# A hybrid decoder layer on one core: output projection by column halves, ring slots loaded during it, normalised rows stored once

## The chip, the cores and the metric

The kernel runs on one core of one Trainium2 chip. The metric is the device time of one launch in microseconds; the medians below are over several launches of the same program. The engines are TensorE (PE; its weight loads are listed as PEld), VectorE (DVE), ScalarE (ACT), GpSimd (POOL) and SyncE (SP, which here issues nearly all transfers). They run their own instruction streams and wait for one another by semaphores.

## What is computed

One layer on x of 512 rows x 1024, all in float32:

```
h = rmsnorm(x, g_mix);  p = h @ w_in                      # 1024 -> 2304 columns
attn = sliding_window_attention(q, k, v, sinks)           # 8 heads x 64, window 128
conv = short_conv(b_gate, c_gate, x_in, conv_w)           # 512 columns, width 3
mix = concat([rmsnorm(attn, g_attn_out), rmsnorm(conv, g_conv_out)])
x = x + mix @ w_out                                       # the output projection
h = rmsnorm(x, g_ffn)
x = x + moe(h, ...)       # top 4 of 32 experts, each 1024 -> 2048 -> 1024, clamped SwiGLU
out = rmsnorm(x, g_final)
```

The experts' weights are 32 x 12 MiB, 403 MB. Each is read once.

## The kernel before

**Stages.** The 512 rows are four row tiles of 128 (TB = 4, index t). First come the norm, the input projection, and attention and convolution in turns, up to about 150 us. Then the output projection with the second norm, the router and the ranks of the tokens within their experts; then 32 experts one after another; then the sum of four expert rows per token and the last norm. The order of every engine's work is written out by hand; there is no scheduler.

**Output projection.** Weights and mixed activations are split in a high and a low part, and three products are summed (high x high, high x low, low x high). For one row tile t and one half n of the 1024 output columns these are 8 chunks of 128 rows of w_out x 3 = 24 matmuls with 512 columns. The accumulators are PSUM banks 2n (attention half) and 2n + 1 (conv half). `out_first` does tile 0, both halves, with the products in another order and the sums of squares (`group_sums`) between them; `out_proj(t, n)` does one half of tile 1, 2 or 3. DVE's `residual(t, n)` adds the result to X. When both halves of a tile are in X, ACT takes the sum of squares (`row_std`), DVE normalises (`second_norm`), PE transposes (`turn_h2`), ACT and DVE copy the two halves of the transposed tile (`turned_h2`), PE multiplies with the router weights (`router`), DVE finds the four chosen experts (`select`), PE sums ranks (`rank`), and DVE takes them over (`place`, `gates`). PE's order is, for t = 1, 2, 3: out_proj(t, 0), turn_h2(t - 1), rank(t - 2), out_proj(t, 1), router(t - 1); then turn_h2(3), rank(2), router(3), rank(3). After that the token lists of the first two experts are summed on PE (`tok_static`, L1163), and POOL fetches their rows with an indirect DMA (L1709).

**Normalised rows in DRAM.** `h2_rows` holds each normalised row four times, once per chosen expert: ACT stores each tile once (L1507, semaphore h2_stored) and then three more copies (L1508, h2_copied). Expert slot lists hold row numbers 4 x token + k, which serve both to fetch h2 rows and to scatter expert results to `expert_rows`. POOL writes the lists with 16 indirect transfers (L1734), reads them back in six (L1739, L1741) and turns row numbers into half and quarter rows (L1745). The third expert's rows and all later ones are fetched through them (L1700, L1703).

**The ring.** Expert weights go through a ring of 16 slots of 1 MiB (2048 floats in each of 128 partitions). Slots 0 to 7 lie in `ring1`, 8 to 11 in `ring2`, 12 to 14 in `mixer`, 15 in `early`. The first product of an expert takes 8 slots (loaded in pairs, L416), the second takes 4 (L421). SP's order is w1 of experts 0 and 1, w2 of expert 0, w1 of expert 2, w2 of expert 1 and so on; for each load after the first 16 slots it waits for PE to have used up the slot (`slot_used`). Until the experts begin, the same memory holds other things: `ring2` the rows of w_out (later their low parts), slots 4 to 7 the high parts, `mixer` q, k, v, gates, attention and conv results, `early` temporaries. So the first 16 slots are gated (`load`, L427): slots 0 to 3 wait for the input projection, 4 to 7 for the end of the output projection (oproj_done 8), 8 to 15 for the first fetched rows (rows_in).

**Experts.** "Big" experts (18 of 32) have 96 rows per pass, small ones 64. PE does for expert i: first product of i, transposition of the rows of i + 1, second product of i - 1, transposition of the activations of i.

Of the kernel before, what the change touches and what calls it, by code (L numbers as in the profile page):

```python
# [59 lines left out]
W_OUT_EARLY = tuple(k for k in range(KT) if k not in W_OUT_LATE)  # L60


W_OUT_PLACES = dict(zip(W_OUT_EARLY + W_OUT_LATE, (6, 7, 4, 5, 0, 1, 2, 3)))

# [10 lines left out]
def layer_kernel(nc, x, g_mix, w_in, conv_w, sinks, g_attn_out, g_conv_out, w_out,  # L75
                 g_ffn, w_router, b_router, w1, b1, w2, b2, g_final, out):
    ctx = ExitStack()
    with ctx:
# [11 lines left out]
        h2_dram = nc.dram_tensor("h2_rows", (ROWS, D), F32).ap()  # L90
# [64 lines left out]
        top8 = sb("top8", [P, 2, 8])  # L155
        top8_i = sb("top8_i", [P, 2, 8], U32)
        top_e = sb("top_e", [P, TB, TOPK])
        top_x = sb("top_x", [P, 2, TOPK])
        rt_small = sb("rt_small", [P, 2, 4])
# [53 lines left out]
        w_out_sb = ring2[:, :].rearrange("p (k n) -> p k n", k=KT)  # L213
        w_out_lo = ring2_r[:, :].rearrange("p (k n) -> p k n", k=KT)

        w_out_hi = ring1_r[:, KT // 2 * SLOT:].rearrange("p (k n) -> p k n", k=KT)
# [4 lines left out]
        kT = mixer[:, 4 * SEQ:6 * SEQ].rearrange("p (g t) -> p g t", g=KV_HEADS)  # L221
        v_sb = mixer[:, 6 * SEQ:7 * SEQ].rearrange("p (t d) -> p t d", t=TB)
        c_gate = mixer[:, 7 * SEQ:8 * SEQ]
        convT = mixer[:, 8 * SEQ:12 * SEQ].rearrange("p (c t) -> p c t", c=CT)
# [4 lines left out]
        convT_lo = mixer_r[:, 2, :].rearrange("p (c t) -> p c t", c=CT)  # L229
# [3 lines left out]
        h2_copies = h2_dram.rearrange("(t p k) n -> t p k n", p=P, k=TOPK)  # L233
# [27 lines left out]
        qkv_in, conv_in, wout_early, wout_late = sem("qkv_in"), sem("conv_in"), sem("wout_early"), sem("wout_late")  # L261
# [24 lines left out]
        h2_turned, h2_stored, h2_copied = sem("h2_turned"), sem("h2_stored"), sem("h2_copied")  # L286
# [83 lines left out]
        def _(sp):  # L370
# [31 lines left out]
            w_out_v = w_out[0].rearrange("(k p) n -> p k n", p=P)  # L402
            sp.wait_ge(part_done, 3 * (CT - 1))
            for k in W_OUT_EARLY:
                sp.dma_start(w_out_sb[:, k, :], w_out_v[:, k, :]).then_inc(wout_early, 16)
            for part, k in enumerate(W_OUT_LATE):
                sp.wait_ge(part_done, 3 * (CT - 1) + part + 1)
                sp.dma_start(w_out_sb[:, k, :], w_out_v[:, k, :]).then_inc(wout_late, 16)
# [18 lines left out]
            def load(i, _parity):  # L427
# [3 lines left out]
                if i >= 2:  # L431
                    ids.append(sp.value_load(order_row[0:1, i:i + 1], min_val=0, max_val=E - 1))
                for k in range(0, KT, 2):
                    n = w1_slot(i, k)
                    if n == 0:
                        sp.wait_ge(part_done, 3 * CT)
                    elif n == KT // 2:
                        sp.wait_ge(oproj_done, 2 * TB)
                    elif n == KT:
                        sp.wait_ge(rows_in, fetches(0))  # L440
                    elif n >= RING:
                        wait_free(n + 1)
                    load_w1(ids[i], k, n % RING)
                if i == 0:
                    return
# [6 lines left out]
            expert_blocks(load)  # L452
# [46 lines left out]
        def _(pe):  # L499
# [119 lines left out]
            def out_parts(t, n, k):  # L619

                half, c = k // CT, k % CT
                rows, cols = slice(t * P, (t + 1) * P), slice(n * 512, (n + 1) * 512)
                return (ps[:, 2 * n + half, :], mixT_hi[:, k, rows], (attnT_lo, convT_lo)[half][:, c, rows],
                        w_out_hi[:, W_OUT_PLACES[k], cols], w_out_lo[:, k, cols])

            def out_first():

                pe.wait_ge(u_ready, CT)
                pe.wait_ge(conv_read, CT)
                for n in range(2):  # L630
                    if n == 0:
                        pe.wait_ge(mix_hi, 1)
                    for order, k in enumerate(W_OUT_EARLY + W_OUT_LATE):
                        if n == 0:
                            pe.wait_ge(wout_hi, order + 1)
                        bank, high, _, w_high, _ = out_parts(0, n, k)
                        mm(bank, high, w_high, start=(k in (0, W_OUT_LATE[-1] + 1)), stop=False)
                    if n == 0:
                        pe.wait_ge(mix_lo, 1)
                    for k in W_OUT_EARLY + W_OUT_LATE:  # L640
                        bank, _, low, w_high, _ = out_parts(0, n, k)
                        mm(bank, low, w_high, start=False, stop=False)
                group_sums()
                for n in range(2):
                    for order, k in enumerate(W_OUT_EARLY + W_OUT_LATE):
                        if n == 0:
                            pe.wait_ge(wout_lo, order + 1)
                        bank, high, _, _, w_low = out_parts(0, n, k)
                        ins = mm(bank, high, w_low, start=False, stop=(k in (CT - 1, W_OUT_LATE[-1])))
                    ins.then_inc(oproj_done, 1)  # L650

            def out_proj(t, n):
# [3 lines left out]
                pe.wait_ge(x2_half, 2 * (t - 1) + n + 1)  # L656
# [1163 lines left out]
```

## Time and profile before

| | us |
|---|---|
| median of 3 runs | 1245.73 (1245.7 to 1246.11) |
| profiled execution | 1248.85 |
| its span, first to last instruction | 1247.3 |
| PE busy | 1159.8 (93%) |
| DVE, ACT, POOL busy | 306.2, 197.6, 172.3 |
| mean rate of all transfers over the span | 369 GB/s |

The page gives busy times as sums over the span; the stages differ, so the sections below use windows (busy time, DMA share and rate in one stretch), waits (who waited for whom) and the timeline (instructions in order of time). "DMA share" is the mean busy share of 16 DMA engines; it can come out a little above 1. "PEclk" is the clock granted to PE, 1.00 being 2.4 GHz and 0.50 being 1.2 GHz. In the timeline, "[2.55 <-DVE normed L1099]" behind a row is the idle time of the engine before it and what ended it, and "x8" means that eight instructions have been merged in one row.

### The profile page before, as it was taken

The page shows a single profiled execution, that of the slowest core. Times are in us where ns is not written, and L with a number is a line of the kernel's source. Part 1 is how long each engine was busy: PE and PEld are TensorE (multiplying, and loading weights), DVE is VectorE, ACT ScalarE, POOL GpSimd, SP SyncE. Part 2 cuts the span into 40 slices and gives each one's busy share as a digit, 9 for nine tenths or more (in the row PEclk, how much of TensorE's full clock was granted, in tenths as well). Part 3 has the DMA queues.
Part 4 walks back from the last instruction along what each step waited for, and adds up shares of the span by engine and source line. Part 5 has one row for each costly group of instructions (what it writes and reads, how often), then busy time and mean ns, then how long its engine had stood idle before and what let it go on. Part 6 is the DMA issues. An engine that isn't in the chain of part 4 may idle for free. (4 is left out here: it accounts for less than half of the span.)

```text
span 1247.3 us, 16600 instructions
## 1 busy us (share of the span) xinstructions
PE 1159.8 (93%) x7030; PEld 483.9 (39%) x7030; DVE 306.2 (25%) x469; ACT 197.6 (16%) x385; POOL 172.3 (14%) x249
## 2 busy tenths in 40 slices
PE   5999998798999999999999898999989899998980
PEld 4777787223333333333333333333333333333330
DVE  4677765420211101101101010110101011010108
ACT  4443623011100100011010000101000010100002
POOL 6000100421111111111111111111111101111000
PEclk9999998798999999999999999999999999999995
DMA  9400655999999999999999999999999999999996
GB/s 334 144 1 11 233 218 224 325 383 403 423 424 424 423 425 423 424 422 425 423 424 423 426 423 423 425 424 423 423 426 424 423 425 422 424 422 425 425 390 243
DMA packets 59247, 460.67 MB, mean 369 GB/s; under 512 B 12439, under 2 KB 12711, under 8 KB 26307
## 3 DMA queue, kind: packets, MB, share of 16 engines
q1 hardware_dynamic: 49362, 434.15, 84.4%
q0 software_dynamic: 7632, 17.05, 3.6%
q10 hardware_dynamic: 2176, 8.39, 1.7%
q8 instruction: 57, 0.93, 0.3%
q14 instruction: 20, 0.16, 0.0%
HBM read 442.58 MB, written 21.41 MB: 372 GB/s over the span
## 5 line engine op out<-in xcount | busy, mean ns | idle before, releaser
L801 PE MATMUL ps<-ring_a,blockT 128*64 128x512 f32 x1472 | 327.2, 595 | 15.6 <-DMA ring_a<-in_w 15.5
L1251 DVE TENSOR_SCALAR xnT<-ps 128x768 f32<-128x768 f32 (+1 forms) x32 | 26.9, 841 | 830.8 <-PE ps L808 522.8
L801 PEld LDWEIGHTS ps<-ring_a,blockT 128*64 128x64 f32 x1472 | 101.0, 137 | 226.8 <-issue 187.7
L827 PE MATMUL ps<-ring_a,actT 128*64 128x512 f32 x736 | 167.2, 601 | 0.0
L1515 ACT ACTIVATE blockT<-ps 128x512 f32<-128x512 f32 x30 | 17.9, 597 | 561.0 <-PE ps L753 561.0
L801 PE MATMUL ps<-ring_b,blockT 128*64 128x512 f32 x448 | 99.9, 595 | 6.9 <-DMA ring_b<-in_w 6.9
L1700 POOL DMA_INDIRECT scores<-h_rows,slots x30 | 31.5, 1049 | 509.8 <-PE ps L753 508.9
L808 PE MATMUL ps<-ring_a,blockT 128*32 128x512 f32 x768 | 87.4, 595 | 0.0
L827 PEld LDWEIGHTS ps<-ring_a,actT 128*64 128x64 f32 x736 | 50.3, 138 | 94.3 <-issue 90.6
L1716 POOL DMA_INDIRECT expert_rows<-normed,slots x32 | 33.2, 1037 | 272.2 <-ACT normed L1544 271.9
L827 PE MATMUL ps<-ring_b,actT 128*64 128x512 f32 x288 | 64.7, 596 | 0.0
L801 PEld LDWEIGHTS ps<-ring_b,blockT 128*64 128x64 f32 x448 | 30.7, 137 | 71.4 <-issue 57.0
L833 PE MATMUL ps<-ring_a,actT 128*32 128x256 f32 x832 | 50.3, 382 | 0.0
L808 PEld LDWEIGHTS ps<-ring_a,blockT 128*32 128x32 f32 x768 | 22.5, 109 | 62.6 <-issue 62.6
L1272 DVE TENSOR_TENSOR xnT<-xnT 128x768 f32<-128x768 f32 (+1 forms) x32 | 42.7, 1333 | 8.8 <-ACT xnT L1538 8.2
L521 PE MATMUL ps<-xnT_hi,ring_r 128*128 128x512 f32 x144 | 39.6, 421 | 4.4 <-ACT ring_r L1357 2.2
L833 PEld LDWEIGHTS ps<-ring_a,actT 128*32 128x32 f32 x832 | 24.4, 109 | 34.5 <-issue 21.1
L525 PE MATMUL ps<-xnT_lo,ring_r 128*128 128x512 f32 x144 | 37.1, 401 | 0.0
L1543 ACT ACTIVATE normed<-ps,slots 128x256 f32<-128x256 f32 x18 | 8.5, 474 | 175.4 <-PE ps L833 175.4
L528 PE MATMUL ps<-xnT_hi,ring_r 128*128 128x512 f32 x144 | 35.6, 389 | 0.0
L1544 ACT ACTIVATE normed<-ps,slots 128x512 f32<-128x512 f32 x32 | 21.9, 684 | 81.8 <-PE ps L827 81.8
L827 PEld LDWEIGHTS ps<-ring_b,actT 128*64 128x64 f32 x288 | 20.0, 136 | 35.9 <-issue 34.8
(297 smaller groups left out, 1077.9 us busy)
## 6 DMA issues: line engine op xcount, KB each, us to landing
ring_a<-in_w SPq DMA_DIRECT2D x98, 2048.0 KB, 32.4
ring_a<-in_w SPq DMA_DIRECT2D x92, 1024.0 KB, 30.4
ring_b<-in_w SPq DMA_DIRECT2D x30, 2048.0 KB, 32.7
ring_b<-in_w SPq DMA_DIRECT2D x36, 1024.0 KB, 33.0
ring<-in_w_in SPq DMA_DIRECT2D x12, 768.0 KB, 19.0
ring<-expert_rows SPq DMA_DIRECT2D x16, 512.0 KB, 15.3
h_rows<-normed ACTq DMA_DIRECT2D x4, 1536.0 KB, 6.5
X<-in_x SPq DMA_DIRECT2D x8, 512.0 KB, 6.2
```

The lines of the kernel that those rows point to most:

```text
L521: mm(ps[:, bank, :], high[:, k, :], xnT_hi[:, k, :], start=(k == 0), stop=False)
L525: mm(ps[:, bank, :], high[:, k, :], xnT_lo[:, :, k, :], start=False, stop=False)
L528: ins = mm(ps[:, bank, :], low[:, k, :], xnT_hi[:, k, :], start=False, stop=(k == KT - 1))
L801: ins = mm(ps[half * HALF:(half + 1) * HALF, b, :], x_of(k)[0], ring(r)[:, 0, at + half * 512:at + (half + 1) * 512], start=False, stop=(k ...
L808: mm(ps[q * QUARTER:(q + 1) * QUARTER, B_BOTH, :], x_of(k)[1], w[:, :, q * 256:(q + 1) * 256], start=False, stop=(k == KT - 1), tile_posit ...
L827: ins = mm(ps[half * HALF:(half + 1) * HALF, bank, :], actT[:, s % 2 * W2_K + j, s // 2 * HALF:(s // 2 + 1) * HALF], ring(r)[:, 0, j * D + ...
L833: ins = mm(ps[q * QUARTER:(q + 1) * QUARTER, bank + 1, 0:256], actT[:, 4 + j, s * QUARTER:(s + 1) * QUARTER], ring(slot(s)[0])[:, 0, j * D ...
L1251: v.tensor_scalar(width(glu_c, big), width(ps_glu, big), LIMIT, None, ALU.min).then_inc(glu_ready, 1)
L1272: v.tensor_tensor(turned.rearrange("p (s k q) -> p s q k", k=W2_K, q=P), a_in.rearrange("p (s q k) -> p s q k", k=W2_K, q=P), b_in.rearran ...
L1544: a.activation(gated_y[:, parity, 0:512], ps[:, bank, :], ACT.Copy, scale=gates[:, HALVES, 1:2].bitcast(F32)).then_inc(y_ready, 1)
L1700: g.indirect_dma_start(gathered[:, 0:512], None, h2_halves, bass.IndirectOffsetOnAxis(lists[:, HALVES, 0:1], 0), bounds_check=last_half_ro ...
L1716: g.indirect_dma_start(y_halves, bass.IndirectOffsetOnAxis(slots[:, HALVES, i, 0:1], 0), gated_y[:, parity, 0:512], None, bounds_check=las ...
```

## The change

1. The output projection goes over all four row tiles for output columns 0 to 511 first, then over all four for columns 512 to 1023. The accumulators are banks 2(t % 2) and 2(t % 2) + 1. Tiles 0 and 1 of the first half are done in `out_first`, in another order of products. `router(0)` and `router(1)` stand in the middle of out_proj(2, 1) and out_proj(3, 1); rank(0), turn_h2(2), rank(1), router(2), turn_h2(3), rank(2), router(3), rank(3) follow. DVE and ACT have new orders to match.
2. w_out is held in chunks of one column half of 256 rows (c = 0 to 3 first half, 4 to 7 second), each run 2 KB instead of 4 KB, and converted in the order 0, 1, 2, 3, 6, 7, 4, 5.
3. In `mixer`, keys, values and gate move to the third slot, conv results to the second. Slots 14 and 15 are loaded after the group sums; 6 to 9 after four half tiles of the projection (oproj_done 4); 4, 5, 10, 11 after all eight; 12 and 13 after the first fetched rows.
4. h2_rows holds each row once. Fetches use token numbers. DVE derives them from the row numbers by a shift (`list_tokens`, after the elementwise work of expert 0), and POOL waits for that and applies two more instructions to get half and quarter rows. The wait for h2_copied is gone.

```diff
             ids = [0, 1]
-            expert_blocks(load)
+
+            def load_first(*slots):
+
+                for n in slots:
+                    e, k = divmod(n, KT)
+                    load_w1(e, k, n)
+
+            sp.wait_ge(part_done, 3 * CT)
+            load_first(0, 2)
+            sp.wait_ge(sums_done, 1)
+            load_first(14)
+            sp.wait_ge(oproj_done, TB)
+            load_first(6, 8)
+            sp.wait_ge(oproj_done, 2 * TB)
+            load_first(4, 10)
+            sp.wait_ge(rows_in, fetches(0))
+            load_first(12)
+            for k in range(W2_SLOTS):
+                wait_free(w2_slot(0, k))
+                load_w2(0, k, w2_slot(0, k) % RING)
+            for i in range(2, E):
+                load(i, i % 2)
...
-                for n in range(2):
-                    if n == 0:
-                        pe.wait_ge(mix_hi, 1)
...
+                high_high(0)
+                low_high(0)
+                high_high(1)
+                high_low(0)
                 group_sums()
...
+                low_high(1)
+                high_low(1)
...
+            out_proj(2, 0)
+            out_proj(3, 0)
+            out_proj(0, 1)
+            out_proj(1, 1)
+            turn_h2(0)
+            out_proj(2, 1, lambda: router(0))
+            turn_h2(1)
+            out_proj(3, 1, lambda: router(1))
+            rank(0)
+            turn_h2(2)
+            rank(1)
+            router(2)
+            turn_h2(3)
+            rank(2)
+            router(3)
+            rank(3)
...
             residual(0, 0)
-            low_mix(2)
+            residual(1, 0)
+            low_mix(3)
+            low_w_out(4)
+            low_w_out(5)
+            residual(2, 0)
+            low_w_out(6)
+            low_w_out(7)
+            residual(3, 0)
             residual(0, 1)
-            low_mix(3)
             second_norm(0)
...
+            residual(1, 1)
+            turned_h2(0)
+            second_norm(1)
+            residual(2, 1)
+            select(0)
+            second_norm(2)
+            turned_h2(1)
+            residual(3, 1)
+            turned_h2(2)
+            second_norm(3)
+            select(1)
+            place(0)
+            place(1)
+            select(2)
+            turned_h2(3)
+            place(2)
+            gates(0)
+            gates(1)
+            gates(2)
+            select(3)
+            place(3)
+            gates(3)
...
+            def list_tokens():
+
+                dve.wait_ge(slots_in, 16 * 6)
+                v.tensor_scalar(slots[:, 2:4, :, 0:1], slots[:, 0:2, :, 0:1], 2, None, ALU.logical_shift_right).then_inc(tokens_ready, 1)
...
-                act.dma_start(h2_copies[t, :, 0, :], normed[:, t % 2, :]).then_inc(h2_stored, 16)
-                act.dma_start(h2_copies[t, :, 1:TOPK, :], normed[:, t % 2, :].unsqueeze(1).to_broadcast([P, TOPK - 1, D])).then_inc(h2_copied, 16)
...
+                act.dma_start(h2_tiles[t, :, :], normed[:, t % 2, :]).then_inc(h2_stored, 16)
...
             pool.wait_ge(slots_in, 16 * 6)
+            pool.wait_ge(tokens_ready, 1)
             for which, factor, col in ((HALVES, 2.0, half_col), (QUARTERS, 4.0, quarter_col)):
-                lines = slots[:, which, :, 0:1]
+                lines, tokens = slots[:, which, :, 0:1], slots[:, 2 + which, :, 0:1]
+                g.tensor_scalar(tokens, tokens, factor, col[:, :], ALU.mult, ALU.add)
                 then(g.tensor_scalar(lines, lines, factor, col[:, :], ALU.mult, ALU.add))
             pool.sem_inc(slots_ready, 1)
             pool.wait_ge(sel_ready, 1)
-            pool.wait_ge(h2_copied, 16 * TB)
```

## Rows read from the trace of the kernel before

**Rows 1.** Windows: stretch, us, each engine's busy us (instructions), PEclk, DMA share, GB/s.

```profile
164.00:205.00 41.00, 41.00 (x209) 33.58 (x207) 23.25 (x59) 12.54 (x23) 0.00 (x0) 1.00 0.39 155
205.00:226.00 21.00, 10.30 (x72) 8.97 (x71) 13.56 (x64) 4.11 (x9) 1.10 (x1) 0.57 0.83 315
226.00:294.00 68.00, 60.50 (x356) 20.03 (x358) 15.52 (x32) 6.07 (x10) 22.77 (x28) 0.88 0.99 375
294.00:1212.00 918.00, 894.72 (x5664) 302.98 (x5662) 115.80 (x153) 89.79 (x172) 119.74 (x123) 1.00 1.01 422
```

**Rows 2.** PE's waits over the whole span: us in total, times, longest.

```profile
PE ps L801 <- DMA ring_a<-in_w: 15.5, 15, 1.8
...
PE ps L801 <- DMA ring_b<-in_w: 6.9, 6, 1.8
PE ps L753 <- DMA scores<-h_rows,slots: 5.0, 1, 5.0
```

**Rows 3.** Waits of SP's queue, 140 to 300 us.

```profile
SPq L416 <- PE ps L661: 56.5, 1, 56.5
...
SPq L416 <- DMA scores<-h_rows,tok_static: 19.9, 1, 19.9
```

**Rows 4.** Timeline of SP's queue: start, us, line, transfers issued.

```profile
226.84 1.48 SPq L416 DMA_DIRECT2D ring_b<-in_w  x2
240.83 3.41 SPq L421 DMA_DIRECT2D ring_a<-in_w  x4
...
266.13 2.07 SPq L416 DMA_DIRECT2D ring_a<-in_w  x2
...
275.73 2.90 SPq L421 DMA_DIRECT2D ring_b<-in_w  x4
293.59 13.92 SPq L416 DMA_DIRECT2D ring_a<-in_w  x4
```

**Rows 5.** Ring loads of L416: issue to landing.

```profile
DMA to landing us min/median/max: 7.9/32.5/38.4
```

**Rows 6.** Timeline of PE, 150 to 227 us.

```profile
152.97 0.50 PE L637 MATMUL ps<-ring_r,xnT_hi 128*128 128x512 f32 x1 [0.44 <-ACT ring_r L1432]
...
164.37 0.47 PE L659 MATMUL ps<-ring_r,xnT_hi 128*128 128x512 f32 x1
...
170.08 1.09 PE L505 MATMUL ps<-ident,normed 128*128 128x128 f32 x8
...
176.91 1.97 PE L694 MATMUL ps<-w_rt,xnT 128*128 128x32 f32 x16
...
213.32 3.62 PE L694 MATMUL ps<-w_rt,xnT 128*128 128x32 f32 x16
218.95 0.21 PE L705 MATMUL ps<-chosen,earlier 128*128 128x32 bf16 x1 [2.01 <-DVE chosen_cum L1120]
```

**Rows 7.** Timeline of DVE, 205 to 221 us.

```profile
205.24 0.75 DVE L1085 SCALAR_TENSOR_TENSOR X<-ps,r_group,X 128x512 f32<-128x512 f32 x1 [3.31 <-PE ps L661]
...
208.32 0.16 DVE L1095 RECIPROCAL stat<-stat 128x1 f32<-128x1 f32 x1 [1.54 <-ACT stat L1339]
...
209.85 0.18 DVE L1111 COPY logit<-ps 128x32 f32<-128x32 f32 x1
...
212.00 0.69 DVE L1104 COPY xnT<-ps 128x512 f32<-128x512 f32 x1 [0.23 <-PE ps L505]
...
220.58 0.16 DVE L1163 TENSOR_SCALAR tok_static<-ps 128x2 int32<-128x2 f32 x1 [0.25 <-PE ps L728]
```

**Rows 8.** Timeline of POOL, 165 to 300 us.

```profile
221.69 1.10 POOL L1709 DMA_INDIRECT scores<-h_rows,tok_static  x1 [70.61 <-DVE tok_static L1163]
...
260.89 1.16 POOL L1739 DMA_DIRECT2D slots<-slot_list  x2 [6.43 <-DMA slot_list<-entry,row_i]
...
273.22 0.29 POOL L1745 TENSOR_SCALAR slots<-slots,half_col 128x32 int32<-128x32 int32 x1 [9.19 <-DMA slots<-slot_list]
...
274.83 1.14 POOL L1700 DMA_INDIRECT scores<-h_rows,slots  x1 [0.92 <-POOL slots L1745]
```

More of the change, by code:

```diff
@@ L59 @@
 W_OUT_LATE = (3, 4, 5)
-W_OUT_EARLY = tuple(k for k in range(KT) if k not in W_OUT_LATE)
-W_OUT_PLACES = dict(zip(W_OUT_EARLY + W_OUT_LATE, (6, 7, 4, 5, 0, 1, 2, 3)))
+W_OUT_EARLY = tuple(c for c in range(KT) if c not in W_OUT_LATE)
+W_OUT_ORDER = (0, 1, 2, 3, 6, 7, 4, 5)
+W_OUT_PLACES = (6, 7, 4, 5, 0, 1, 2, 3)
 def head_place(h):
@@ L621, in out_parts, with high_high, low_high, high_low @@
                 half, c = k // CT, k % CT
-                rows, cols = slice(t * P, (t + 1) * P), slice(n * 512, (n + 1) * 512)
-                return (ps[:, 2 * n + half, :], mixT_hi[:, k, rows], (attnT_lo, convT_lo)[half][:, c, rows],
-                        w_out_hi[:, W_OUT_PLACES[k], cols], w_out_lo[:, k, cols])
+                rows, chunk = slice(t * P, (t + 1) * P), n * CT + k // 2
+                return (ps[:, 2 * (t % 2) + half, :], mixT_hi[:, k, rows], (attnT_lo, convT_lo)[half][:, c, rows],
+                        w_out_hi[:, W_OUT_PLACES[chunk], k % 2, :], w_out_lo[:, chunk, k % 2, :])
+            def high_high(t):
+                pe.wait_ge(mix_hi, t + 1)
+                for k in range(KT):
+                    if t == 0 and k % 2 == 0:
+                        pe.wait_ge(wout_hi, k // 2 + 1)
+                    bank, high, _, w_high, _ = out_parts(t, 0, k)
+                    mm(bank, high, w_high, start=(k % CT == 0), stop=False)
+            def low_high(t):
+                pe.wait_ge(mix_lo, t + 1)
+                for k in range(KT):
+                    bank, _, low, w_high, _ = out_parts(t, 0, k)
+                    mm(bank, low, w_high, start=False, stop=False)
+            def high_low(t):
+                for k in range(KT):
+                    if t == 0 and k % 2 == 0:
+                        pe.wait_ge(wout_lo, k // 2 + 1)
+                    bank, high, _, _, w_low = out_parts(t, 0, k)
+                    ins = mm(bank, high, w_low, start=False, stop=(k % CT == CT - 1))
+                ins.then_inc(oproj_done, 1)
             def out_first():
@@ L643, in out_first @@
-                group_sums()
[L644 to L652, printed above, removed]
+                high_high(0)
@@ L1068, in _ @@
             low_mix(0)
-            for order in range(2, KT):
-                low_w_out(order)
-                if order == 3:
-                    attended(TB - 1)
+            low_w_out(2)
+            low_w_out(3)
             low_mix(1)
+            attended(TB - 1)
+            low_mix(2)
             dve.wait_ge(gstd_ready, 1)
```

225 lines of the change are left out of this document (102 added, 123 removed).

## Prediction, made before the change was run

> **What bounds the kernel now.** I read the windows first. From 294 to 1212 us the DMA share is 1.01 at 422 GB/s while PE is busy 895 of 918 us [rows 1]: the expert phase is paced by the weight stream. PE's waits say the same: its stops for the ring sum to 15.5 + 6.9 us, 1.8 us at most each [rows 2]. So PE follows the DMA closely, with about 22 us of its own in reserve. One ring slot (1 MiB) is 1.049 MB / 422 GB/s = 2.49 us of stream; everything below is counted in that.
>
> Ahead of the experts the stream is not full: share 0.39 in 164 to 205 us, 0.83 in 205 to 226 [rows 1]. The DMA queue's waits name the two gates: 56.5 us for the last output-projection matmul (L661), 19.9 us for the first fetched rows [rows 3]. That is the idle time the change wants to use. When the fetched rows land, at 226.8, 8 of the 16 slots are requested and landed; the other 8 are requested at once [rows 4].
>
> The next question is which limit follows once the gates open. The DMA cannot hold more than 16 slots ahead of PE. Between 226 and 294 us it moved 375 GB/s x 68 us = 25.5 MB [rows 1]. About 1.3 MB of that is fetched rows and the rest of the row stores (two fetches of 96 rows of 4 KB, one of 128 half rows, some 0.3 MB of stores), so 24.2 MB or 23 slots are weights; with the first 8 that is 31 of the 32 requested by then, since slots 32 and 33 are requested only at 293.6 [rows 4]. **Before the change the ring is already all but caught up at 293.6 us**; only after that does the stream fall behind its requests for good. A head start given earlier can survive only as far as PE frees slots earlier.
>
> **The change, part by part.**
>
> *Preloaded slots.* At the moment the rows land, 14 slots are in instead of 8: six slots, 6 x 2.49 = 14.9 us of stream moved into idle time. What remains of it: the last pair before that (12, 13) takes 5 us, and then the queue waits for PE to free slot 0, which before happens at 240.8 [rows 4]; from there each request follows PE. In the old time scale, with the shift of the whole phase kept apart, slots 24 and 25 are requested at 266.1, the four slots 28 to 31 from 275.7 on [rows 4]. From rest a pair lands 7.9 us after its request [rows 5], of which 5.0 is transfer, so 2.9 is start-up. Slots 24 to 31 are then in at 266.1 + 2.9 + 8 x 2.49 = 288.9, with a fetch of half rows 289.4. Before, the 32nd slot landed at 293.6 + 1.1 x 2.49 = 296.3. So the stream is 6.9, say 7.0 us ahead of the old one there, not 14.9: the rest is lost as idle DMA behind a full ring. This holds only if PE too gets on: slots 32 and 33 must be requested by about 287, and before they were at 293.6 because PE stood 5.0 us for its third fetch [rows 2] and then ran slowly.
>
> *The third fetch.* Its chain on POOL: list reads issued from 260.9 on after 6.4 us of waiting, their landing waited for 9.2 us more, index arithmetic at 273.2, fetch issued at 274.8 [rows 8]. All of it ran beside a stream that never paused. In the new kernel the ring is dry around 264 to 269, so the list reads land sooner; against that stand one DVE shift and two more POOL instructions, 0.3 us each by the row at 273.2, and the wait for DVE (behind the shift on POOL stands the whole of its queue; DVE is free by then and idle until the next product). The wait of 5.0 can end between 0 and 6; I take 0.7 us left. Row against rule: what the rows show is small transfers slow beside the stream [rows 8]. The Trainium skill, "DMA: Bandwidth & Descriptors", section "Queues, rings and completion order", says each engine takes turns between its queues packet by packet; by that a list read pays for a busy stream however short its backlog is. With the reads beside a busy stream the rule would leave the wait at 5 us and the sum 4.3 higher, near 1251; no row before shows a list read beside an idle stream, so it can't be checked here.
>
> *The projection in PE's order.* The same 48 + 144 matmuls of 512 columns run; a block of 24 takes 5.7 us (164.4 to 170.1) [rows 6]. Out of the stretch before the last of them goes one transposition of 0.9 us and the 0.4 us wait for a weight half at 152.9 [rows 6], since only four chunks are now needed first. A new stall comes in: the second router stands in the middle of the last block. Adding up in the new order: the first 48 + the sums end at 164.0 instead of 164.4; five blocks of 5.65, one transposition and one router (1.97 us for its products [rows 6], 2.15 with its bias) bring the end of the block of tile 2, half 1, to 195.3; another transposition and half a block reach the middle of the last block at 199.0. But DVE has behind that tile's residual (two of 0.75) first the choice of tile 0 (1.9), then the norm of tile 2 (1.6), and only then the copy that the router needs (0.7): 195.3 + 0.1 + 1.5 + 1.9 + 1.6 + 0.7 = 201.1 [rows 7]. Stall 2.1 us; it can be between 0 (if DVE were always in time) and 3. The last matmul moves by -0.9 - 0.4 + 2.1 = +0.8.
>
> *The tail behind the last matmul.* This is the largest cost. Before: last residual at 205.2; norm from 208.3, over at 209.85 where the choice of tile 2 begins (until 211.8, 1.9 us); copy at 212.0 to 212.7; router 3 at the slow clock, 3.62 us for its products instead of 1.97; last rank 218.95, so that 4.3 us lie between the copy's end and choice 3 (218.95 - 1.9 - 212.7); token list 220.6, 1.6 behind the rank [rows 6, 7]. That is 15.4 us from the residual to the list. In the new order, from the residual at zero: norm until 4.6 as before (the copy of tile 2 hides under the squares); then DVE does choice 1 (1.9) and placing 0 (taken as half of the 1.6, 0.8) before PE can go on, which waits with rank 1 ahead of router 2: 7.3. Router 2 at the slow clock 4.2: 11.5. Choice 2 1.9, with the transposition of tile 3 beside it on PE: 13.4. Copy 0.7, router 3 4.3: 18.4. Choice 3 1.9 and 1.6 from rank to list: 22.0 with the hand-overs. So the tail is 22.0 against 15.4: +6.6. It has two routers in a row where one was. The clock is 0.57 in 205 to 226 [rows 1], the lower of the two levels (1.2 and 2.4 GHz), in a stretch where PE was busy 10.3 of 21 us; I take it so for the new tail too, which has more waiting. At the fast clock the two routers would save 1.65 us each by their products, some 4 us with bias and transposition; that is the lower bound, 2.6; the upper one is 8, with a microsecond and a half more of hand-overs.
>
> *Row stores.* 8.4 MB become 2.1 MB. They run in 170 to 226 us where the DMA has room, and no instruction but the norm of a tile two later waits for them, so nothing on the path; only the first fetch no longer shares the engines with the last three quarters of copies. It was issued at 221.7 and had landed at 226.8 at the latest [rows 4, 8]; I take 0.4 of that off, between 0 and 1.5.
>
> *Free of charge.* The moved places of keys, values and conv rows change no instruction; weight chunks of 2 KB runs in place of 4 KB are 4 MB in all and landed with time to spare, bounded by the 0.4 us that PE waited for one [rows 6] below and 1 us above; POOL's bounds registers are set while it idles. The overflow branch isn't entered before, and its added waits cost nothing then.
>
> **Sum.** Stream ahead -7.0; projection +0.8; tail +6.6; first fetch -0.4; rest of the third fetch's wait +0.7: +0.7 us. The profiled execution took 1248.85 us, its span 1247.3; the runs' median, 1245.7, lies 3.1 below, and the shift is carried over unchanged: 1246.4 us. Bounds of the likeliest case: the wait wholly gone and the slow stretch behind it too -2.5, first fetch -1.5, stall 2.1 shared with the tail -1; against that +2 on the third fetch: 1242.5 to 1249.
>
> **Rivals.**
> (1) *The head start is kept.* The 14.9 us of stream count in full against +7.0 of later start: -7.9, 1238. For it: PE has 22 us of waits on the ring [rows 2]. Against it: 31 of 32 slots were in at 293.6.
> (2) *The tail costs little*, if PE keeps the fast clock or DVE gets to the choices sooner: tail +2 to +4 in place of 6.6, 1242 or less. Against it: clock 0.57 already now.
> (3) *The stalls pile up: slower.* PE stops for 2.1 us within the last block. If the granted clock falls to the lower level at that stop, as it did in the tail [rows 1], the 5 us of work left take up to 3.4 more. And if the list reads miss the dry stretch, slots 32 and 33 come 5 us late, +4.5. One of them gives 1250, both 1254. It decides from the point where later start and late requests together exceed the 7 us of head start by 2.5.
> (4) *It doesn't do what it says*: the early loads are held up, for instance because their gates open no earlier. Each gate is an earlier event than the one it replaces (group sums, then four finished half tiles instead of eight), so I give this nothing; by the argument of the full ring it would cost up to those 7 us.
>
> **How the numbers follow.** What the measurement can tell from no change is about 0.2%, 2.5 us. Chances: likeliest case 0.43, (1) 0.12, (2) 0.10, (3) 0.35. The range leaves out 0.1 on each side: half of (1) and more below, the end of (3) above: 1239.5 to 1253. Faster 0.23 (both faster rivals, a little of the likeliest), same 0.42, slower 0.35.
>
> **What would show it.** In the windows of the changed kernel: DMA share near 1 in parts of 164 to 205, near 0 for some microseconds between 238 and 248, full from about 276 on. In the queue's timeline slot 0's second use is requested near 248, slots 32 and 33 near 295. PE's timeline: last projection matmul 0.8 us later, two routers of 3.6 us behind it, token list near 228. PE's wait for the third fetch under 2 us. If the first expert matmul does not come 6 to 8 us later than 229, the tail is wrong; if slots 32 and 33 come 7 us later than 293.6 with the stream waiting for them, the third fetch is. PE's waits for the ring should stay near 22 us if the stream still paces all.

## The result: slower by 0.43%, and the profile after

The changed kernel took 1251.24 us in the median (6 runs, 1250.05 to 1254.99), the kernel before 1246.44 beside it (1245.70 to 1247.03): ratio 1.0043, 95% interval 1.0030 to 1.0056. Slower, by 4.8 us. The two profiled executions lie closer: 1250.5 against 1248.85 us, spans 1248.9 against 1247.3. What follows explains these 1.6 us first. The other 3.2 us come from where the two profiled executions lie among the runs, which is taken up at the end.

The windows of the changed kernel (columns as in [rows 1]):

```profile
164.00:205.00 41.00, 38.59 (x191) 32.07 (x190) 21.45 (x37) 5.42 (x11) 0.00 (x0) 0.98 0.45 178
200.00:205.00 5.00, 4.80 (x26) 4.24 (x27) 0.00 (x0) 0.15 (x1) 0.00 (x0) 0.81 0.27 107
205.00:226.00 21.00, 13.35 (x62) 11.72 (x61) 10.97 (x46) 4.75 (x12) 0.00 (x0) 0.58 0.58 225
226.00:294.00 68.00, 57.62 (x379) 19.94 (x381) 22.48 (x73) 6.46 (x12) 25.90 (x31) 0.89 0.76 279
245.00:250.00 5.00, 5.00 (x42) 1.22 (x36) 0.00 (x0) 0.00 (x0) 3.78 (x5) 1.00 0.31 20
270.00:275.00 5.00, 5.00 (x40) 1.28 (x38) 0.00 (x0) 0.00 (x0) 2.50 (x5) 1.00 0.82 282
294.00:1212.00 918.00, 893.58 (x5655) 302.17 (x5652) 116.19 (x153) 88.17 (x169) 118.09 (x122) 1.00 1.01 423
```

From 294 us on nothing differs: 423 GB/s, and the waits below for the ring are 17.7 + 6.4 us against 15.5 + 6.9 [rows 2]. Between 245 and 250 us the queue is dry (20 GB/s): the ring is full. The wait of 5.0 us for the third fetch [rows 2] is gone, and one of 6.4 us for the ranks is new.

PE's waits over the whole span:

```profile
PE ps L838 <- DMA ring_a<-in_w: 17.7, 15, 1.8
...
PE ps L737 <- DVE ranks L1173: 6.4, 1, 6.4
PE ps L838 <- DMA ring_b<-in_w: 6.4, 5, 1.8
```

SP's queue in the kernel before, at the first fetched rows (one row more than [rows 4], where the third request behind them, 226.84, is the first one shown):

```profile
226.00 0.81 SPq L416 DMA_DIRECT2D ring_a<-in_w  x2
```

and in the changed kernel:

```profile
234.45 0.33 SPq L421 DMA_DIRECT2D ring_b<-in_w  x1
247.86 2.90 SPq L426 DMA_DIRECT2D ring_a<-in_w  x4
259.46 15.86 SPq L421 DMA_DIRECT2D ring_a<-in_w  x4
282.76 2.90 SPq L426 DMA_DIRECT2D ring_b<-in_w  x4
293.98 13.92 SPq L421 DMA_DIRECT2D ring_a<-in_w  x4
```

The request at 293.98 is that of slots 32 and 33, at 293.59 before. This request is a good yardstick: in all 14 profiles of this case the span ends 952.9 to 955.0 us behind it. So all but some 2 us is decided ahead of it, and a profile can be read as a chain of marks. The table gives, in us of the span, the start of the last residual and of the token list on DVE, SP's first request behind the first fetched rows, and its first requests for w2(0) (slot 16), slot 20, w2(1) (slot 28) and slots 32, 33. It includes profiles of the experiments told below:

| kernel, profile | last residual | token list | first rows in | w2(0) requested | slot 20 | w2(1) | slots 32, 33 | span |
|---|---|---|---|---|---|---|---|---|
| before | 205.24 | 220.58 | 226.00 | 240.83 | 252.43 | 275.73 | 293.59 | 1247.3 |
| changed | 206.97 | 229.11 | 234.45 | 247.86 | 259.46 | 282.76 | 293.98 | 1248.9 |
| e3_both | 201.39 | 219.62 | 224.99 | 239.54 | 251.14 | 274.44 | 285.66 | 1238.9 |
| e4_late | 209.76 | 231.90 | 237.25 | 251.02 | 262.62 | 285.92 | 305.75 | 1258.6 |
| e9, before again | 204.94 | 219.97 | 225.44 | 240.68 | 258.42 | 281.72 | 292.94 | 1247.0 |
| e10, changed again | 206.87 | 229.00 | 234.31 | 247.57 | 267.80 | 291.13 | 302.35 | 1256.2 |
| e11, e3 again | 203.38 | 222.19 | 227.48 | 241.39 | 259.99 | 283.29 | 294.51 | 1249.5 |

Differences between the first two lines: the last residual +1.7 us; from there to the list 22.1 instead of 15.3, +6.8; list to rows -0.1; rows to w2(0) -1.4; then two equal steps; and from w2(1) to slots 32, 33 11.2 instead of 17.9, -6.6. Sum +0.4, and 1.2 more behind the yardstick. So the change costs 8.5 us and gains 8.1. The -1.4 are the clock: the first 32 matmuls of the first product take 8.08 us instead of 9.50, since the granted clock is back at its upper level sooner behind their start. These 32 before, then in the changed kernel:

```profile
230.19 9.50 PE L801 MATMUL ps<-ring_a,rowsT 128*64 128x512 f32 x32
```

```profile
238.65 8.08 PE L838 MATMUL ps<-ring_a,rowsT 128*64 128x512 f32 x32
```

### The profile page after: what moved, and what is told of

The parts are those of the page before. It is cut to its first block and busy times, and to the rows that moved or that the text cites. A ratio compares the mean times of both kernels' runs of the same rounds, so it can differ in the third digit from the quotient of the medians.

```text
span 1248.9 us, 16593 instructions
## 1 busy us (share of the span) xinstructions
PE 1157.7 (93%) x7030; PEld 485.2 (39%) x7030; DVE 306.9 (25%) x470; ACT 191.6 (15%) x378; POOL 171.7 (14%) x251
## 5 line engine op out<-in xcount | busy, mean ns | idle before, releaser
L838 PE MATMUL ps<-ring_a,blockT 128*64 128x512 f32 x1472 | 327.3, 595 | 17.9 <-DMA ring_a<-in_w 17.7
L1586 ACT ACTIVATE blockT<-ps 128x512 f32<-128x512 f32 x30 | 17.9, 597 | 558.5 <-PE ps L790 558.5
L845 PEld LDWEIGHTS ps<-ring_a,blockT 128*32 128x32 f32 x768 | 22.5, 109 | 62.6 <-issue 62.6
## 6 DMA issues: line engine op xcount, KB each, us to landing
ring<-in_w_in SPq DMA_DIRECT2D x12, 768.0 KB, 18.6
```

Of the source, the lines that this page charges most:

```text
L838: ins = mm(ps[half * HALF:(half + 1) * HALF, b, :], x_of(k)[0], ring(r)[:, 0, at + half * 512:at + (half + 1) * 512], start=False, stop=(k ...
L845: mm(ps[q * QUARTER:(q + 1) * QUARTER, B_BOTH, :], x_of(k)[1], w[:, :, q * 256:(q + 1) * 256], start=False, stop=(k == KT - 1), tile_posit ...
```

## The experiments

The experiments ran on three chips: e1 to e4 on one (call it A; kernel before 1247.68 us there), e5 to e8 on B (1249.40), e9 to e12 on C (1249.49). Ratios are to the kernel before on the same chip. The changed kernel itself did not run on A or B; its 1.0043 is from the first chip.

**The stop in the last block and the tail, apart and together.** PE's timeline of the changed kernel shows both places:

```profile
197.41 0.39 PE L692 MATMUL ps<-ring_r,mixer_r 128*128 128x512 f32 x1
200.20 0.40 PE L724 MATMUL ps<-b_rt,ones_row 1*128 1x32 f32 x2 [2.41 <-ACT xnT L1546]
...
202.89 0.40 PE L692 MATMUL ps<-ring_r,mixer_r 128*128 128x512 f32 x1
203.12 0.59 PE L690 MATMUL ps<-ring_r,xnT_hi 128*128 128x512 f32 x1
203.52 0.63 PE L691 MATMUL ps<-ring_r,xnT_hi 128*128 128x512 f32 x1
203.94 0.63 PE L692 MATMUL ps<-ring_r,mixer_r 128*128 128x512 f32 x1
...
214.33 0.18 PE L737 MATMUL ps<-chosen,earlier 128*128 128x32 bf16 x1 [6.45 <-DVE ranks L1173]
...
215.03 3.62 PE L726 MATMUL ps<-w_rt,xnT 128*128 128x32 f32 x16
...
221.84 3.62 PE L726 MATMUL ps<-w_rt,xnT 128*128 128x32 f32 x16
227.48 0.21 PE L737 MATMUL ps<-chosen,earlier 128*128 128x32 bf16 x1 [2.02 <-DVE chosen_cum L1156]
```

PE stops for 2.41 us ahead of router(1), and 3 us after it has gone on the distance between matmuls goes from 0.23 to 0.43 us: the granted clock has fallen to the lower level (0.81 over 200 to 205 us above). Nine matmuls at 0.2 us more are 1.8 us. Then comes 6.45 us for rank(1), which needs the choice of tile 1, with the next router queued behind it, and two routers at the slow clock, 3.62 us each.

e1 takes router(2) ahead of rank(1). The condition that held it back was the buffer of the logits, freed by the whole choice; it gets a signal of its own:

```diff
-                elif t >= 2:
-                    pe.wait_ge(chosen_ready, t - 1)
+                else:
+                    pe.wait_ge(logits_read, t)
...
-            rank(1)
             router(2)
+            rank(1)
...
             residual(3, 1)
+            read_logits(1)
             turned_h2(2)
             second_norm(3)
-            select(1)
+            select(1, False)
             place(0)
-            place(1)
             select(2)
+            place(1)
```

> Changed kernel, but router 2 stands ahead of rank 1 on PE (and choice 2 ahead of placing 1 on DVE), and DVE reads the logits of tile 1 out of PSUM right behind the last residual. PE's wait of 6.4 us for the placing of tile 0 should shrink to about 2. Theory A (the later start of the experts is passed on one for one, because the ring is full before they begin): token list 2.8 us earlier, time 1251.2 - 2.8 = 1248.4. Theory B (the head start of the weight stream covers a later start, the loss is elsewhere, in the expert phase): token list earlier too, but time unchanged within 1 us, 1251.

Measured: 1247.80 us, ratio 1.0003 (0.9990 to 1.0016), near theory A's 1248.4. The wait of 6.45 us is gone; in its place stands one of 2.67 us ahead of router(2), and residual to list takes 18.2 us instead of 22.1. But in this execution the clock fell already at router(1) (3.62 us for its products), and the last residual came at 209.06.

e2 leaves the tail alone and lets DVE and ACT serve router(1) first (with e1's signal for the logits):

```diff
             residual(2, 1)
-            select(0)
-            second_norm(2)
+            read_logits(0)
             turned_h2(1)
+            select(0, False)
+            second_norm(2)
...
             squares_h2(2)
-            store_h2(2)
             turned_h2(1)
+            store_h2(2)
```

> Changed kernel, but DVE and ACT copy the transposed tile 1 right behind the residual and squares of tile 2, before choice 0 and the norm of tile 2. The stop of 2.4 us ahead of router 1 goes; if the granted clock then stays at its upper level, the nine matmuls behind it take 0.23 us instead of 0.43 us each, 1.8 us more. Theory A: 1251.2 - 4.2 = 1247.0. Theory B: unchanged, 1251. Third reading (the clock falls there in any case, by the router and transposition themselves): -2.4 only, 1248.8.

Measured: 1245.80 us, ratio 0.9988 (0.9979 to 0.9996). PE no longer stops, the granted clock is 1.00 over 200 to 205 us, and the last residual comes at 203.21: 3.8 us sooner, more than the stop of 2.41. The clock no longer falls there, which is the other part. Residual to list stays at 22.5.

e3 is both edits.

> Both edits together. Theory A: token list some 7 us earlier than in the changed kernel, level with that of the kernel before; time 1251.2 - 7 = 1244.2, which would be 2 us faster than before: what the head start is worth when the experts begin no later. If the head start were worth its full 14.9 us, 1246.4 - 14.9 = 1231.5. Theory B: 1251.

Measured: 1240.83 us, ratio 0.9959 (0.9944 to 0.9975). The list comes at 219.62 in place of 229.11, 9.5 us sooner, and the span is 10.0 us shorter. Of the 9.5 us, 3.9 are the tail and some 4 the stop with its clock; 1.6 lie ahead of both edits, where this execution was already early (router(0) at 187.75 against 189.38). Against the kernel before, w2(0) is requested 1.3 us sooner and the step from w2(1) to slots 32, 33 is 6.6 us shorter: on this chip the early loads do bring their 7 us, once nothing takes them back. The version is 0.4% faster than the kernel before, and by the ratios faster than the changed one. Two of its 12 runs took 1248.4 and 1249.0.

**What the early loads are worth, and through what.** e4 is the changed kernel with the first ring slots gated as before:

```diff
-            sp.wait_ge(sums_done, 1)
-            load_first(14)
-            sp.wait_ge(oproj_done, TB)
-            load_first(6, 8)
             sp.wait_ge(oproj_done, 2 * TB)
-            load_first(4, 10)
+            load_first(4, 6)
             sp.wait_ge(rows_in, fetches(0))
-            load_first(12)
+            load_first(8, 10, 12, 14)
```

> Changed kernel with the first ring slots gated as before: 0 to 3 behind the input projection, 4 to 7 behind all of the output projection, 8 to 15 behind the first fetched rows. Everything else as changed. Theory A (ring full, most of the head start lost as idle stream): the kernel before plus the later start of 7.6 us, 1254, so 3 us slower than the changed kernel, at most 7. Rival (the head start counts in full): 14.9 us slower, 1266. PE should wait about 5 us for the third fetch again, because the list reads run beside a busy stream.

Measured: 1258.05 us, ratio 1.0079 (1.0066 to 1.0093); span 9.7 us longer than the changed kernel's. 2.8 us of that lie ahead of the last residual: the stop is 2.41 us as before, but the clock fell already at router(1) (3.62 us for its products), as in e1, which has the early loads. From w2(1) to slots 32, 33 it is then 19.8 us instead of 11.2, +8.6, and behind the yardstick 2.1 us less. Theory A had said 1254, at most 1258. The 8.6 us begin with one row of PE:

```profile
295.75 1.12 PE L786 MATMUL ps<-ident,scores 128*128 128x128 f32 x4 [6.59 <-DMA scores<-h_rows,slots]
...
297.70 5.89 PE L860 MATMUL ps<-ring_a,actT 128*64 128x512 f32 x16
```

Of the 6.59 us, 1.05 are a wait for ACT that the changed kernel has in the same place; 5.5 are the late rows, and the product behind them takes 5.89 us instead of 3.65 at the lower clock. So the early loads act through the third fetch. Its chain on POOL, in the changed kernel and in e4 (start, us, line, idle before):

```profile
269.36 1.16 POOL L1812 DMA_DIRECT2D slots<-slot_list  x2 [6.41 <-DMA slot_list<-entry,row_i]
...
276.03 0.29 POOL L1819 TENSOR_SCALAR slots<-slots,half_col 128x32 int32<-128x32 int32 x1 [3.54 <-DVE slots L1326]
...
278.26 1.14 POOL L1773 DMA_INDIRECT scores<-h_rows,slots  x1 [0.89 <-POOL slots L1820]
```

```profile
271.18 1.17 POOL L1808 DMA_DIRECT2D slots<-slot_list  x2 [5.41 <-DMA slot_list<-entry,row_i]
...
284.49 0.29 POOL L1815 TENSOR_SCALAR slots<-slots,half_col 128x32 int32<-128x32 int32 x1 [10.16 <-DVE slots L1322]
```

From the list reads' issue to the first use it is 6.7 us in the changed kernel, whose stream all but runs out meanwhile, 13.3 us in e4, whose stream does not pause, and 12.3 before [rows 8]. The stream in the changed kernel, then in e4:

```profile
273.00:274.00 1.00, 1.00 (x13) 0.26 (x8) 0.00 (x0) 0.00 (x0) 0.00 (x0) 1.00 0.25 65
```

```profile
275.00:277.00 2.00, 2.00 (x24) 0.65 (x20) 0.00 (x0) 0.00 (x0) 0.00 (x0) 1.00 1.01 417
```

The 8 KB list reads land, in the median, 3.4 us after their issue in the changed kernel, 8.3 in e4 and 7.8 before. These 6.6 us more are enough to make the fetch late by 5.5. The Trainium skill, "DMA: Bandwidth & Descriptors", section "Queues, rings and completion order", has the engines take turns between queues packet by packet. The two chains are in keeping with that, since the reads are slow only while the other queue has work; the turns themselves they don't show.

**A second effect, which none of my theories had.** The next four kernels ran on chip B. Each is e3 with one edit. e5 has e4's edit, the gates of before.

> The kernel of e3 (both edits of the order) with the first ring slots gated as before: 0 to 3, then 4 to 7 behind all of the projection, 8 to 15 behind the first fetched rows. In the profiles so far, request of slot 32 to the end of the span was 953 to 955 us in all six; it came 59.5 to 61 us behind the first fetched rows with early loads and 67 to 68 us without. Theory A (the early loads are worth about 7 us, by the third fetch no longer being late, whatever the order of the projection): 1240.8 + 7 = 1248, PE waiting 5 to 6.6 us for the third fetch. Rival (they are worth more once the experts begin early, up to 14.9 us): up to 1256.

e6 stands half way between e3 and e5:

```diff
-            sp.wait_ge(sums_done, 1)
-            load_first(14)
             sp.wait_ge(oproj_done, TB)
-            load_first(6, 8)
+            load_first(6)
             sp.wait_ge(oproj_done, 2 * TB)
-            load_first(4, 10)
+            load_first(4, 8)
             sp.wait_ge(rows_in, fetches(0))
-            load_first(12)
+            load_first(10, 12, 14)
```

> The kernel of e3 with 10 slots in when the first rows land instead of 14: 6 and 7 behind the first column half, 4, 5, 8, 9 behind the whole projection, 10 to 15 behind the first rows. If what counts is the backlog of the stream beside the list transfers (a shorter backlog lets them land sooner), the wait for the third fetch comes back in part: 1243 to 1246. If it counts only whether the ring is dry when the lists are read, it comes back whole: 1248. If two slots of lead are enough: 1241.

e7 puts a delay on POOL ahead of the third fetch (4.0 us by its row):

```diff
+            for _ in range(16):
+                then(g.iota(pad[:, :], [[1, 64]], base=0, channel_multiplier=0, allow_small_or_imprecise_dtypes=True))
```

> The kernel of e3 with 16 chained iota instructions of 128x64 on POOL ahead of the third fetch, some 5 to 6 us, nothing else. The weight stream keeps its whole head start. Theory A (until slot 32 is requested PE's pace sets the time, since the ring is full): PE waits some 4 to 5 us for the third fetch, its clock falls to the lower level, slot 32 is requested some 6 us later, and the time is 1240.8 + 6 = 1247. Theory D (the head start of the stream itself is what was gained, and carries over a late fetch): 1241 to 1242.

e8 takes one more router forward, with ACT's order to match:

```diff
-            rank(2)
             router(3)
+            rank(2)
...
+            read_logits(2)
             turned_h2(3)
+            select(2, False)
```

> The kernel of e3 with a shorter tail: PE does router 3 ahead of rank 2, DVE reads the logits of tile 2 and copies the transposed tile 3 ahead of choice 2, ACT copies the transposed tile 2 ahead of the squares of tile 3. From last residual to token list 18.2 us in e3; worked out 16.7. Theory A: 1240.8 - 1.5 = 1239.3. If the loads of 4, 5, 10, 11 or the fetch then collide: no gain.

Measured: e5 1251.77 (ratio 1.0010, 0.9999 to 1.0022), e6 1251.28 (1.0013, 1.0002 to 1.0024), e7 1251.65 (1.0018, 1.0004 to 1.0031), e8 1250.77 (1.0009, 1.0001 to 1.0018). Four kernels with very different loads, and all within 1.0 us. All lie 3 us or more above the times worked out from e3's 1240.8. The wait for the third fetch appeared in none, not in e5 with the late loads and not in e7 with the delay. e8's tail is no shorter either (residual to list 19.0 us; PE waits 3.1 us for the last choice instead of 2.1). All four profiles have instead, in the first expert's first product, PE advancing by single matmuls with idle time that nothing releases, and w2(0)'s four requests take 9.8 to 11.3 us where e3 took 2.9. The last four kernels are there to tell a property of these kernels from one of the chip: before, changed and e3 again, and e12, the kernel before with the "stored once" half of the change alone:

```diff
-                act.dma_start(h2_copies[t, :, 0, :], normed[:, t % 2, :]).then_inc(h2_stored, 16)
-                act.dma_start(h2_copies[t, :, 1:TOPK, :], normed[:, t % 2, :].unsqueeze(1).to_broadcast([P, TOPK - 1, D])).then_inc(h2_copied, 16)
+                act.dma_start(h2_tiles[t, :, :], normed[:, t % 2, :]).then_inc(h2_stored, 16)
```

> The kernel before, unchanged, for a second profile and more times beside the three kernels of this job. The four profiles of e5 to e8 have in the first expert's first product, at 248 to 257 us, matmuls 1 to 2 us apart with idle time that nothing in the profile releases, and the four requests of w2(0)'s slots take 9.8 to 11.3 us where e3_both took 2.9; those kernels ran on another chip than e1 to e4. Theory C (the stall belongs to the chip or the execution and strikes any kernel): if the other profiles of this job have these gaps, this one has them too, and the time is 1247 to 1254. Theory K (the stall belongs to kernels that reach the first product before about 235 us): no gaps here, 1247.5 within 1.5, slot 32 requested at 293 to 296 us, and the wait for the third fetch is there with 4 to 6.5 us.

> The changed kernel, unchanged. The first profile differs from that of the kernel before by 1.6 us, the medians by 4.8, and two of its six times are 4 us above the rest. Tail theory: 1.0043 within 0.0015 of the kernel before, slot 32 requested at 294 to 298 us, no wait for the third fetch, the 6.45 us wait for rank(1) and a stall of 2.4 us ahead of router(1) as in the first profile. Theory C adds: if the profile has gaps of up to 1.5 us without a releaser in the first product, the four requests of w2(0) take about 10 us, slot 32 is requested at 300 to 303 us, and the time is 1255 to 1258. Theory K: no such gaps, since its first product begins at 242 us.

> e3_both again, unchanged: the changed kernel with the router products issued ahead of the rank products, and residual(2,1) and the first turning ahead of the selection. It gave 1240.83 us, 0.9959 of the kernel before, with 2 of 12 runs near 1248.5. If what slowed e5 to e8 came with the chip or the execution (theory C), this is 1240.8 within 1.5 where the profile has the four requests of w2(0) in 3 us, and 1248 to 1251 where they take 10 us, slot 32 then requested at 293 to 295 us instead of 285.7. If e5 to e8 were slow by their own edits, it is 0.996 within 0.0015 of the kernel before on any chip, and without gaps.

> The kernel before with only the second half of the change: each normalised row is stored once (the queue of the normalised rows carries 2.1 MB instead of 8.4), the fetches divide the slot number by four, and the selection does not wait for the copies. In the forecast this was worth nothing ahead of the first expert and up to 0.7 us at the third fetch (a division on DVE and POOL between list and fetch). Theory of the forecast: 1.0000 to 1.0008 of the kernel before (0 to +1 us). Rival: the copies, written beside the stream, hold it back by up to 6.3 MB at 420 GB/s, 15 us of the queues, of which the dry time of 20 us hides some; without them slots 12 to 19 land sooner and the time is 2 to 5 us lower.

Measured on chip C: before again 1248.64 us (ratio 0.9991, 0.9979 to 1.0002, the kernel against itself), changed again 1259.95 (1.0091, 1.0068 to 1.0114, four runs), e3 again 1251.04 (1.0015, 1.0003 to 1.0026), stored once 1250.76 (1.0005, 0.9993 to 1.0017). Theory C holds (the stall comes with the chip or the execution, not with one kernel): all four profiles have it. PE in e9, the unchanged kernel before:

```profile
242.56 5.82 PE L801 MATMUL ps<-ring_a,rowsT 128*64 128x512 f32 x25
248.54 1.08 PE L801 MATMUL ps<-ring_a,rowsT 128*64 128x512 f32 x3 [0.16 <-issue]
249.92 1.38 PE L801 MATMUL ps<-ring_a,rowsT 128*64 128x512 f32 x3 [0.31 <-issue]
252.05 0.59 PE L801 MATMUL ps<-ring_a,rowsT 128*64 128x512 f32 x1 [0.74 <-issue]
253.47 1.03 PE L808 MATMUL ps<-ring_a,rowsT 128*32 128x512 f32 x2 [0.83 <-issue]
254.88 0.59 PE L808 MATMUL ps<-ring_a,rowsT 128*32 128x512 f32 x1 [0.38 <-issue]
256.28 3.65 PE L808 MATMUL ps<-ring_a,rowsT 128*32 128x512 f32 x29 [0.81 <-issue]
...
286.01 0.63 PE L753 MATMUL ps<-ident,scores 128*128 128x128 f32 x4 [1.05 <-ACT actT L1517]
...
287.13 3.65 PE L827 MATMUL ps<-ring_a,actT 128*64 128x512 f32 x16
```

and in e10, the unchanged changed kernel:

```profile
249.94 7.37 PE L838 MATMUL ps<-ring_a,rowsT 128*64 128x512 f32 x32
258.35 1.32 PE L845 MATMUL ps<-ring_a,rowsT 128*32 128x512 f32 x2 [1.03 <-issue]
261.16 1.86 PE L845 MATMUL ps<-ring_a,rowsT 128*32 128x512 f32 x3 [1.50 <-issue]
263.29 6.08 PE L845 MATMUL ps<-ring_a,rowsT 128*32 128x512 f32 x27 [0.27 <-issue]
```

The step from w2(0)'s request to slot 20's prices it: 11.60 us in every profile without the stall (before, changed, e1 to e4), 17.7 in e9, 20.2 in e10, 18.6 in e11, 19.1 in e12, so 6.1, 8.6, 7.0 and 7.5 us. Now follow the table. In e9 the stall's 6.1 us cost nothing: the third fetch lands meanwhile, its wait of 5.0 us is gone, the product behind it takes 3.65 us instead of 5.52, and slots 32, 33 are requested at 292.94, even 0.65 us sooner. In e10 there is no such wait left to hide it, and the request comes at 302.35 instead of 293.98. **The kernel before loses 6.6 us at the third fetch, and the stall can hide in them; the change has already taken them out.** Early loads and stall remove the same wait, and it can be removed only once. e5 and e11, e3 with late loads on B and with early loads on C, fit: with the stall their requests for slots 32, 33 lie at 295.40 and 294.51, and the ratios are 1.0010 and 1.0015. On B itself the early loads of e7 and e8 bring nothing over e5 either (1.0018 and 1.0009). e7's delay of 4.0 us falls into the time that the stall gives the fetch and so says nothing of the fetch.

e12 answers its own question too: storing the rows once moves neither w2(0) (241.49 against e9's 240.68, 0.4 of it there already at the last residual) nor the time, and the rival of 2 to 5 us less is out. What the shift and the longer index arithmetic cost at the third fetch can't be seen there, because the stall hides that wait too.

## Why the prediction held, and where it did not

The forecast was 1246.4 us and no change (0.42), range 1239.5 to 1253. The time, 1251.2, lies within the range, but outside the likeliest case (given as 1242.5 to 1249; its listed bounds add up to 1241.4 and 1248.4). The sign is that of rival 3 (0.35), and one of its two conditions came, the clock falling at the stop. That the time lies near that rival's 1250, and inside the range, is in part luck: the clock's part was 1.8 us of its 3.4, and 3.2 of the 4.8 us come from the profiles' distance to the medians. By steps:

- *Projection +0.8*: mis-sized. Measured +1.7, and +2.3 from the same point of the attention ahead of it (147.86 against 148.44 us), since this execution was 0.6 us early. The stop was forecast at 2.1 us and took 2.41; the clock falling at it, which I had put into rival 3 at up to 3.4 us, took 1.8. In e1, e4 and e10 it fell sooner, and the products of router(1) took 3.62, 3.62 and 3.21 us instead of 1.97. e2 shows stop and clock to be one cost of 3.8 us. I should have carried the clock's part in the sum: the stop in the tail before already stood beside a lower clock.
- *Tail +6.6*: right. 22.0 us forecast, 22.1 measured, with the wait for rank(1) and two routers of 3.62 us. e1 and e3 show 4 us of it to be the order of rank and router alone.
- *First fetch -0.4*: measured -0.1 (list to rows 5.3 us instead of 5.4), at the edge of its bounds. The 226.8 at which I had the rows land is the third request behind them; the first is at 226.00. With the rows stored once and nothing else changed it is 5.5 (e12), so fewer copies bring nothing here.
- *First product*: nothing forecast, -1.4 measured, the clock that comes back sooner behind its start.
- *Stream ahead -7.0, rest of the third fetch +0.7*: the size is right, by way of the sum: w2(1) to slots 32, 33 is 6.6 us shorter. The full ring is there (20 GB/s at 245 to 250 us), the head start of 14.9 us was not kept (rival 1), and the request forecast near 295 came at 293.98. The list reads hit a stretch in which the stream all but ran out (65 GB/s at 273 to 274 us, not the 264 to 269 forecast), so rival 3's +4.5 did not come; the wait fell to nothing instead of 0.7. The 1251 that stood beside a wait of 5 us fits the time by its number alone. But the -7.0 was booked as stream ahead and the fetch as a remainder. e4 shows one mechanism: the gain is the fetch's wait and the slow product behind it, no more.
- *Behind slots 32, 33*: nothing forecast, +1.2 measured (954.9 against 953.7), with 1.7 us more of waits for the ring; that is inside the scatter of the 14 profiles, 952.9 to 955.0.
- *Row stores 0*: right as far as seen (e12: ratio 1.0005, interval 0.9993 to 1.0017, with the stall).
- *From the profile to the median*: the step that failed. I carried the profiled execution's distance to the median over unchanged. The two profiles differ by 1.6 us, the medians by 4.8 on the first chip and by 10.5 on C (1259.95 against 1249.49). On C the reason is shown: the stall costs the changed kernel 8.4 us at the yardstick and the kernel before none. On the first chip the profile of the kernel before was 2.4 us slower than the median of its runs and slower than all six, and that of the changed kernel 0.7 us faster; 1.65 + 2.41 + 0.74 gives the 4.8. Why they lay so is open. The changed kernel's two runs at 1254.4 and 1255.0, about 4 us above the other four, suggest executions with a stall among ones without, but no profile caught one there, and without these two its median would still be 1250.4, 4.0 us above the kernel before.

Rival 4 is out: the ring is full at 245 us. Rival 2 is out as well: the clock was 0.58 over 205 to 226 us, and the tail 6.8 us longer.

Which version is best depends on the stall. e3_both beats the changed kernel on C, where both ran (1251.04 against 1259.95 us, 0.7%), and by the ratios of A and the first chip (0.9959 against 1.0043). Against the kernel before it wins 0.41% on A and loses 0.15% on C.

## What to carry to other kernels

A wait that the profile shows may be hiding another delay: before counting its removal as a gain, ask what else hides in it, and profile the kernel before on more than one chip, more than once. Price a stop of TensorE in front of dense work with the slower matmuls behind it, here 2.4 + 1.8 us, and when one accumulator is reused, signal its read and not the end of the work on it. A mark late in the chain with a constant distance to the end (here the request of one ring slot) splits every further profile into steps that can be compared; take care that each mark is the same event in both kernels.

## What the runs showed of the hardware

- PE can stall in dense float32 matmuls with nothing in the profile that it waits for. The stall begins behind matmul 87 to 96 of the first product's 128, at 248 us in e9 and at 257 in e10, so it goes with the work and not with the time since the start; it costs 6 to 9 us and lets single matmuls through with gaps of up to 1.5 us. All eight profiles on chips B and C have it, none of the six of the first run's chip and A. The PEclk column stays at 1.00 over 248 to 268 us in e5, e8, e9 and e11; over 248 to 260 us it is 0.72 in e12, 0.81 in e6 and 0.86 in e7, and over 260 to 268 us 0.57 in e10, so a lower clock can come with the stall but isn't needed for it. One 16 KB instruction transfer falls near the same place with and without the stall (248 to 252 us in before and e9, 252 to 258 in the changed kernel and e10), so the runs don't tell whether it is power, instruction supply or something else.
- Reads of slot lists of 8 KB landed 8.3 us after their issue beside a stream of 417 GB/s (e4), 3.4 us where the stream all but ran out meanwhile (changed kernel), and 1.9 us in e10, where the stall had left the queue nearly idle.
- The same program on one chip spread by 5 us from run to run (before on A 1244.1 to 1249.4), where the first three runs lay within 0.4 us; the clock's fall around router(1) came behind its products in the changed kernel, within them in e10 and ahead of them in e1 and e4, with a stop of 2.4 to 2.5 us each time.
